# Six feature blocks ahead of the first projection, and one first phase of two passes

## The chip, the cores and the metric

The kernel runs on one core of a Trainium2 chip. The metric is the device time of one execution in microseconds (us), the median of three runs. The engines are TensorE (PE: matmuls and transposes, PEld: weight loads beside them), VectorE (DVE), ScalarE (ACT), GpSimd (POOL) and SyncE (SP), which issues nearly all transfers from the chip's memory (HBM) to the on-chip memory (SBUF). Matmuls write into eight banks of PSUM.

## The reference

Two transformer blocks on 256 tokens of width 2048, in float32. The first mixes with two kinds of attention (stick-breaking, and sparse with an indexer that keeps the 64 best keys per query), the second with gated linear attention (GLA); each has a gated feed-forward part. What matters here is the beginning of the first block:

```python
c_act = jax.nn.silu(c)
mod = c_act @ w_ada[l] + b_ada[l]                 # 2048 x 12288
sh1, sc1, gt1, sh2, sc2, gt2 = jnp.split(mod, 6, axis=-1)
h = modulate(rms_norm(x, g_mix[l]), sh1, sc1)     # h * (1 + sc1) + sh1
z = h @ w_in[l]                                   # 2048 x 11344
(q_sb, k_sb, v_sb, q_ds, k_ds, v_ds, q_ix, k_ix, w_ix,
 gate_sb, gate_ds) = split_columns(z)             # 1024 wide each, k_ix 64, w_ix 16, gates 2048
o_sb = stick_breaking_attention(q_sb, k_sb, v_sb) # 8 heads
o_ds = indexer_sparse_attention(q_ds, k_ds, v_ds, q_ix, k_ix, w_ix * (N_IDX_HEADS ** -0.5), rel_bias)
merged = (jax.nn.sigmoid(gate_sb) * (o_sb @ w_o_sb[l])
          + jax.nn.sigmoid(gate_ds) * (o_ds @ w_o_dsa[l]))
x = x + gt1[:, None, :] * (merged @ w_out[l])
...                                               # feed-forward with sh2, sc2, gt2, then the second block
```

So no projection can start before the columns of w_ada for sh1 and sc1 have been read and summed, at least those of the features that the projection multiplies first.

## The kernel before

**Halves.** All large weights come through one path. A half is 512 KB of weights: two blocks of 128 features by 512 columns. SP reads it into one of eight places of `raw` (L294 or, in the first phase, L335), ScalarE rounds it to a high part `whi` (L1014), VectorE subtracts to get the low part `wlo` (L1586), and TensorE multiplies the 256 tokens with 12 matmuls of 512 columns: high by high, high by low, low by high (`half`, L472, its matmuls L482 to L484). There are 896 halves. `whi` and `wlo` have four places, so the two splitting engines can be four halves ahead of TensorE; SP issues a half's transfer once the low part of the half eight before is made (`lo_made`). Two halves are a slab.

**The modulation.** c @ w_ada is done on VectorE: one row block of w_ada at a time is multiplied by its entry of c_act and added to a sum (L1681 and L1691 for the first columns, L1702 for later ones, L1606 for the rest). The sums over 128 partitions are then turned into columns by small matmuls with ones (`first_columns`, L567). For sh1 and sc1 the 16 feature blocks stand in two parts: the first EARLY = 10 blocks come in 16 pieces of 1280 KB (`early_piece`, L321) ahead of any projection, the other six in 16 pieces of 768 KB (`late_piece`, L327) beside the first halves. The pieces go through SLOTS = 4 places.

**The phases.** A (48 halves) computes q, k, v of the stick-breaking part in six groups of 512 columns: a first pass over the ten early blocks of all six groups (30 halves), then a second over the other six blocks (18 halves). Partial sums that don't fit into PSUM are drained after the first pass and added after the second. B (4 x 16 halves) computes q, k, v of the sparse part and the queries of the indexer; beside its halves the eight stick-breaking heads run, one per eight halves. C1 (32 halves, from half 112 on, slabs 56 to 71) computes the first gate, and beside it the indexer's scores are added up; in its last slabs eight rounds of top-k (L1866, L1867) run on VectorE, one per half split. C2 (32 halves from half 144 on, slabs 72 to 87) computes the second gate beside the sparse heads: scores, softmax on VectorE (`soft`, which ends at L1903), turned probabilities (L709), values. O, U and the feed-forward parts follow.

**The other w_ada columns.** The columns for sh2, sc2, gt1 and gt2 come in chunks of 512 KB (`ada_chunk`, L306, two places), added by L1606. A table, CHUNKS_AT, says after which slab SP issues which chunk; the add stands in VectorE's program behind the split of that slab's second half. SP waits, before it issues chunk n, for the add of chunk n - 2, and all that SP issues is one line of instructions.

**The distance loads.** `hankels` (L374) is 16 loads of bias tables per head from a small DRAM scratch (L380, L382), in SP's line after a slab of C1; the sparse heads' softmax uses them.

**Warming up.** Ahead of the first projection TensorE runs matmuls whose result is not used (`keep_running`, L573), between the transposes of X (L516) and the column sums.

Of the kernel before, what the change touches and what calls it, by code (L numbers as in the profile page):

```python
# [37 lines left out]
for _h in range(GH):  # L38
# [43 lines left out]
def build_program(nc, A, out):  # L82
# [205 lines left out]
    def _(sp):  # L288
# [57 lines left out]
        for i in range(48):  # L346
            first_half(i)
            if i == 2 * RING - 1:
                for kt in range(SLOTS):
# [4 lines left out]
            if i == 28:
                sp.dma_start(ixw_raw[:].rearrange("p (k n) -> p k n", k=KT), w_in[:, :, C_IX:C_IX + NIXW]).then_inc(sem("ixw_in"), 16)
            if i % 2:
                for n in CHUNKS_AT.get(i // 2, ()):
# [107 lines left out]
    def _(pe):  # L465
# [2138 lines left out]
```

## Time and profile before

| | us |
|---|---|
| runs | 2686.44, 2686.55, 2687.0; median 2686.55 |
| profiled execution, span | 2684.8 |
| TensorE busy | 2629.5 (98%) |
| VectorE busy | 1794.2 (67%) |
| ScalarE busy | 1290.9 (48%) |
| first projection matmul | starts at 70.06 |

The profile is of one execution. Its times count from the start of the span, which is the time from the first to the last instruction that it shows; a run's time is a little longer. The granted clock is the share of full speed at which TensorE was allowed to run. An idle time in brackets stands behind the engine that had it, with what ended it; a wait of TensorE is one that its matmuls had, and SPq is SP's issuing of a transfer, not the transfer.

### The profile page before, as it was taken

Reading aid. Unit: us, or ns where it says so; the run is one execution under the profiler, and the core shown is the slowest. Engines: PE = TensorE matmul, PEld = TensorE weight load, DVE = VectorE, ACT = ScalarE, POOL = GpSimd, SP = SyncE. Lnnn points to the kernel's source line nnn. Section 1 sums busy time; section 2 is a strip of 40 time slices with the busy share of each in tenths; the row PEclk is TensorE's granted clock in tenths of the full one; section 3 lists DMA queues with packets and bytes.
Section 4 is the critical chain, followed back from the end, with each engine's and each line's share of the span. In section 5 each row is a group of like instructions: output and inputs, shape, how many; then the busy total and the mean of one; then the engine's idle time right before and its main releaser. Section 6 shows DMA issues by size and latency. Waiting matters only on the chain.

```text
span 2684.8 us, 34364 instructions
## 1 busy us (share of the span) xinstructions
PE 2629.5 (98%) x12051; PEld 2166.7 (81%) x12051; DVE 1794.2 (67%) x2061; ACT 1290.9 (48%) x1558; POOL 228.6 (9%) x164
## 2 busy tenths in 40 slices
PE   2999999999999999999999999999999999999999
PEld 1887887888888888888888887887888888888887
DVE  7977776878777666666666865677555555555554
ACT  2545554445455444444444564556554444444443
POOL 0000000100000000000000310130001111111110
PEclk9999999999999999999999999999999999999999
DMA  9978777677786666666666556643666666666663
GB/s 391 389 269 301 270 259 256 209 251 264 291 286 230 205 202 205 202 204 203 203 203 189 188 172 184 190 145 126 203 186 191 188 192 190 188 192 190 189 194 134
DMA packets 280529, 585.56 MB, mean 218 GB/s; under 512 B 21776, under 2 KB 24236, under 8 KB 279540
## 3 DMA queue, kind: packets, MB, share of 16 engines
q1 hardware_dynamic: 280084, 583.61, 67.0%
q8 instruction: 58, 0.95, 0.1%
q10 hardware_dynamic: 352, 0.71, 0.1%
q14 instruction: 35, 0.29, 0.0%
HBM read 582.07 MB, written 2.11 MB: 218 GB/s over the span
## 4 chain that ended last, share of the span: by engine, by line
PE 94%; DVE 3%; DMA 1%; issue 1%; ACT 0%; SPq 0%; DVEq 0%; ACTq 0%
PE lin L482 29%; PE lin L484 29%; PE lin L483 29%; DVE sb_acc L1681 1%; DMA sb_raw<-in_w_in_dram 1%; PE aux L785 1%; DMA sb_ada<-in_w_ada_dram 1%; PE aux L516 1%; PE aux L959 0%; PE aux L573 0%; PE aux L796 0%; DVE sb_wlo L1586 0%; PE aux L482 0%; PE aux L484 0%; PE aux L483 0%
## 5 line engine op out<-in xcount | busy, mean ns | idle before, releaser
L1586 DVE TENSOR_TENSOR sb_wlo<-sb_raw,sb_whi 128x1024 fp32r<-128x1024 f32 x896 | 1103.6, 1236 | 781.0 <-ACT sb_whi L1014 777.6
L1014 ACT ACTIVATE sb_whi<-sb_raw 128x1024 fp32r<-128x1024 f32 x896 | 948.0, 1060 | 1219.6 <-PE lin L484 1134.9
L482 PE MATMUL lin<-sb_whi,sb_act_hi 128*128 128x512 f32 x2636 | 1045.1, 396 | 1.8 <-DVE sb_wlo L1586 1.0
L484 PE MATMUL lin<-sb_whi,sb_act_lo 128*128 128x512 f32 x2636 | 1027.4, 390 | 0.0
L483 PE MATMUL lin<-sb_wlo,sb_act_hi 128*128 128x512 f32 x2636 | 1026.3, 389 | 0.0
L482 PEld LDWEIGHTS lin<-sb_whi,sb_act_hi 128*128 128x128 f32 x2636 | 495.2, 188 | 107.0 <-issue 8.7
L484 PEld LDWEIGHTS lin<-sb_whi,sb_act_lo 128*128 128x128 f32 x2636 | 494.7, 188 | 104.6
L483 PEld LDWEIGHTS lin<-sb_wlo,sb_act_hi 128*128 128x128 f32 x2636 | 495.5, 188 | 100.2 <-issue 2.2
L482 PE MATMUL lin<-sb_whi,sb_hid_hi 128*128 128x512 f32 x704 | 275.4, 391 | 0.0
L484 PE MATMUL lin<-sb_whi,sb_hid_lo 128*128 128x512 f32 x704 | 274.2, 389 | 0.0
L483 PE MATMUL lin<-sb_wlo,sb_hid_hi 128*128 128x512 f32 x704 | 273.9, 389 | 0.0
L484 PEld LDWEIGHTS lin<-sb_whi,sb_hid_lo 128*128 128x128 f32 x704 | 132.1, 188 | 27.7
L483 PEld LDWEIGHTS lin<-sb_wlo,sb_hid_hi 128*128 128x128 f32 x704 | 132.2, 188 | 27.0
L482 PEld LDWEIGHTS lin<-sb_whi,sb_hid_hi 128*128 128x128 f32 x704 | 132.2, 188 | 27.0
L1606 DVE SCALAR_TENSOR_TENSOR sb_ada_acc<-sb_ada_in,sb_small,sb_ada_acc 128x1024 f32<-128x1024 f32 x90 | 115.1, 1279 | 0.7 <-DVE sb_u_lo L1659 0.7
L2489 POOL TENSOR_TENSOR sb_yacc<-sb_yacc,sb_dstage 128x512 f32<-128x512 f32 x36 | 55.6, 1545 | 556.8 <-ACT sb_dstage L1028 556.8
L2489 POOL TENSOR_TENSOR sb_x<-sb_x,sb_dstage 128x512 f32<-128x512 f32 x36 | 63.6, 1766 | 336.3 <-ACT sb_dstage L1028 336.3
L2468 POOL TENSOR_TENSOR sb_hank<-sb_hank,sb_selneg 128x384 f32<-128x384 f32 x8 | 11.7, 1492 | 516.4 <-DVE sb_selneg L1880 516.4
L2495 POOL TENSOR_TENSOR sb_ubuf<-sb_ubuf,sb_cacc 128x512 f32<-128x512 f32 x11 | 18.1, 1647 | 397.7 <-ACT sb_ubuf L1028 397.7
L2097 DVE SCALAR_TENSOR_TENSOR sb_cacc<-sb_gpad,sb_par,sb_cacc 128x256 f32<-128x256 f32 x88 | 48.1, 588 | 5.7 <-DVE sb_cacc L2097 1.4
L482 PE MATMUL lin<-sb_whi,sb_u_hi 128*128 128x512 f32 x128 | 51.0, 398 | 0.0
L484 PE MATMUL lin<-sb_whi,sb_u_lo 128*128 128x512 f32 x128 | 49.9, 390 | 0.0
(360 smaller groups left out, 1804.8 us busy)
## 6 DMA issues: line engine op xcount, KB each, us to landing
sb_raw<-in_w_in_dram SPq DMA_DIRECT2D x176, 512.0 KB, 5.9
sb_raw<-in_ffn_w_gu_dram SPq DMA_DIRECT2D x176, 512.0 KB, 3.7
sb_ada_in<-in_w_ada_dram SPq DMA_DIRECT2D x128, 512.0 KB, 4.1
sb_raw<-in_gla_w_in_dram SPq DMA_DIRECT2D x96, 512.0 KB, 3.8
sb_raw<-in_w_gate_dram SPq DMA_DIRECT2D x88, 512.0 KB, 3.8
sb_raw<-in_w_up_dram SPq DMA_DIRECT2D x88, 512.0 KB, 4.4
sb_raw<-in_w_down_dram SPq DMA_DIRECT2D x88, 512.0 KB, 5.6
sb_raw<-in_ffn_w_down_dram SPq DMA_DIRECT2D x88, 512.0 KB, 3.6
```

The lines of the kernel that those rows point to most:

```text
L482: pe.matmul(o, h, whi[:, w], start=first and q == 0, stop=False)
L483: pe.matmul(o, h, wlo[:, w], start=False, stop=False)
L484: m = pe.matmul(o, l, whi[:, w], start=False, stop=last and q == 1)
L516: m = pe.transpose(aux[n % 4][:, q * S + tb * P:q * S + (tb + 1) * P], src[:, tb, (2 * g + q) * P:(2 * g + q + 1) * P], ident)
L785: m = pe.transpose(aux[f // 2][:, f % 2 * S + tb * P:f % 2 * S + (tb + 1) * P], src[:, tb, f * P:(f + 1) * P], ident)
L1014: act.activation(whi[:, idx % RING * HALF:(idx % RING + 1) * HALF], raw[:, idx // 2 % RING, idx % 2 * HALF:(idx % 2 + 1) * HALF], ACT.Copy ...
L1586: dve.tensor_tensor(wlo[:, c], raw[:, idx // 2 % RING, idx % 2 * HALF:(idx % 2 + 1) * HALF], whi[:, c].bitcast(fp32), ALU.subtract).then_i ...
L1606: dve.scalar_tensor_tensor(acc[:, c], ada_in[:, half, :], cact[:, ds(kt, 1)], acc[:, c], ALU.mult, ALU.add).then_inc(sem("ada_sum"), 1)
L1681: m = dve.scalar_tensor_tensor(acc, new, cact[:, kt:kt + 1], acc, ALU.mult, ALU.add)
L2097: m = dve.scalar_tensor_tensor(cacc[:, f, :], gpad[:, f, 2 - k:2 - k + S], col(w, f), cacc[:, f, :], ALU.mult, ALU.add)
L2489: pool.tensor_tensor(y[:, 0, s], y[:, 0, s], dstage[:, c % 2, :], ALU.add).then_inc(sem("dstage_free"), 1)
L2495: pool.tensor_tensor(ubuf[:, 0, :], ubuf[:, 0, :], cacc[:].rearrange("p a t -> p (a t)")[:, 0:NB], ALU.mult).then_inc(sem("up_mul"), 1)
```

## The change

EARLY goes from 10 to 6 and SLOTS from 4 to 6. The early pieces have 768 KB; the ten late blocks come in 32 half rows of 640 KB (sh1 and sc1 apart) beside halves 4 to 35, in six places. Phases A and B become one phase A of 112 halves in 14 groups: a first pass over three pairs of blocks for all groups (42 halves), a second over the other five pairs (70 halves). The heads stand in the second pass, one per seven halves from half 55 on. The third column sum has 40 small matmuls with 16 columns, before 24 with 32, and comes after half 38, before after half 25. Partial sums of the first pass are both drained on ScalarE and both added on VectorE. The `ada_columns` sums move from the end of B into C1, after its halves 13 and 15. `hankels` comes after slab 68, before after slab 64. The table of chunks is another one. The scaling of X comes after the add of block 6, before of block 7.

```diff
-EARLY = 10
+EARLY = 6
-SLOTS = 4
+SLOTS = 6
+LATE_SLOTS = 6
...
-    ("A", 1, 48, 9), ("B", 4, 16, 2), ("C1", 1, 32, 4), ...
+    ("A", 1, 112, 25), ("C1", 1, 32, 4), ...
...
-LATE_AT = {}
-for _k in range(KT):
-    LATE_AT.setdefault(A_PAIRS + 4 * _k // 3, []).append(_k)
+LATE_SUMMED = 38
+LATE_PAIRS = 41
+HEADS_AT = [55 + 7 * _h for _h in range(NH)]
...
 for _n in range(110):
-    _at = 14 + _n * 10 // 16 if _n < 16 else 24 + (_n - 16) * 6 // 7 if _n < 44 else 4 + _n if _n < 64 else 11 + _n if _n < 96 else 13 + _n if _n < 107 else 17 + _n
+    _at = 23 + _n * 33 // 20 if _n < 20 else 56 + (_n - 20) // 2 if _n < 32 else 62 + (_n - 32) * 44 // 64 if _n < 96 else 13 + _n if _n < 107 else 17 + _n
...
-        def late_piece(kt):
-
-            sp.wait_ge(sem("ada0_sum"), EARLY_ROWS if kt < SLOTS else EARLY_ROWS + kt - SLOTS + 1)
-            sp.dma_start(ada1[:, kt % SLOTS, :].rearrange("p (b n) -> p b n", b=2), w_first[kt * P:(kt + 1) * P, :, EARLY * P:D]
-                         ).then_inc(sem(f"ada0_in{kt % SLOTS}"), 16)
+        def late_piece(n):
+
+            kt, b = n // 2, n % 2
+            if n >= LATE_SLOTS:
+                sp.wait_ge(sem("ada0_sum"), EARLY_ROWS + n - LATE_SLOTS + 1)
+            else:
+                if n == 0:
+                    sp.wait_ge(sem("tt_T"), KT // 2)
+                sp.wait_ge(sem("ada0_sum"), KT - SLOTS + n + 1)
+            sp.dma_start(ada1[n % LATE_SLOTS][:], w_ada[kt * P:(kt + 1) * P, b * D + EARLY * P:(b + 1) * D]).then_inc(...)
...
-                if after and s == 0:
+                if after and s == 4:
                     after()
...
-            acc, c0, w = (acc1, 0, KT - EARLY) if n == 2 else (acc0, k0 * P, k1 - k0)
+            acc, c0, w, wide = (acc1, 0, KT - EARLY, WIDE // 4) if n == 2 else (acc0, k0 * P, k1 - k0, WIDE // 2)
...
+        for i, (g, p) in enumerate(A_HALVES):
+            again = i >= A_FIRST
...
+            if i == LATE_SUMMED:
+                pe.wait_ge(sem("ada0_sum"), EARLY_ROWS + 2 * KT)
+                first_columns(2)
+            if i == A_ENDS[0] - 1:
+                project_ix()
+            if i == A_ENDS[1]:
+                wix_turn()
+            for h, at in enumerate(HEADS_AT):
+                if i == at:
+                    sb_turn(h)
+                if i == at + 2:
+                    sb_scores(h)
+                if i == at + 5:
+                    sb_suffix(h)
+                if i == at + 7:
+                    sb_values(h)
...
+            if idx in (13, 15):
+                pe.wait_ge(sem("sb_out"), NH)
+                ada_columns(idx // 15)
...
-            if kt == 7:
+            if kt == 6:
                 norm_stats(0)
                 norm_rows(X)
...
         def a_sum(n):
 
             drained(0, "A", A_ENDS[n])
             for tb, free in ((0, free0), (1, free1)):
-                dve.wait_ge(free, 2 + 3 + n)
-                z = sbz[:, tb, g * NB:(g + 1) * NB]
-                dve.tensor_tensor(z, banks[tb][:], z, ALU.add).then_inc(free, 1)
+                dve.wait_ge(free, 2 + GROUPS - A_HELD + n)
+                z = projected(A_AGAIN[n], tb)
+                dve.tensor_tensor(z, lin[n % 2][tb][:], z, ALU.add).then_inc(free, 1)
...
+        for n in range(2 * KT):
+            hk.setdefault(RING + n, []).append(lambda n=n: late_add(n))
```

On SP, at the start: w_ada pieces (`sb_ada`), the first halves (`sb_raw`) and X (`sb_x`) before,

```order
L321 DMA sb_ada_56<-in_w_ada_dram 128x2x1280 x4
L341 DMA sb_x<-in_x_dram 128x2x2048
...
L321 DMA sb_ada_56<-in_w_ada_dram 128x2x1280 x12
L335 DMA sb_raw<-in_w_in_dram 128x2x512 x8
L327 DMA sb_ada_57<-in_w_ada_dram 128x2x768 x4
L335 DMA sb_raw<-in_w_in_dram 128x2x512 x6
L327 DMA sb_ada_57<-in_w_ada_dram 128x2x768
```

and now:

```order
L328 DMA sb_ada_56<-in_w_ada_dram 128x2x768 x4
L353 DMA sb_x<-in_x_dram 128x2x2048
...
L328 DMA sb_ada_56<-in_w_ada_dram 128x2x768 x12
L347 DMA sb_raw<-in_w_in_dram 128x2x512 x5
L340 DMA sb_ada_0_57<-in_w_ada_dram 128x1280
L347 DMA sb_raw<-in_w_in_dram 128x2x512
L340 DMA sb_ada_1_58<-in_w_ada_dram 128x1280
```

The early pieces are shorter, and from the fifth half on a half row of the late columns stands between every two halves.

On SP, in C1 around the distance loads (`sb_hank`; a row of `sb_raw` x2 is a slab, a row of `sb_ada_in` its chunk): before, the slab ahead of the loads is halves 128 and 129, the one behind them 130 and 131,

```order
L294 DMA sb_raw<-in_w_in_dram 128x2x512 x2
L306 DMA sb_ada_in<-in_w_ada_dram 128x1024
L294 DMA sb_raw<-in_w_in_dram 128x2x512 x2
L306 DMA sb_ada_in<-in_w_ada_dram 128x1024
L380 DMA sb_hank<-bias_by_distance 128x256
...
L294 DMA sb_raw<-in_w_in_dram 128x2x512 x2
```

and now halves 136 and 137, and 138 and 139:

```order
L299 DMA sb_raw<-in_w_in_dram 128x2x512 x2
L313 DMA sb_ada_in<-in_w_ada_dram 128x1024
L299 DMA sb_raw<-in_w_in_dram 128x2x512 x2
L313 DMA sb_ada_in<-in_w_ada_dram 128x1024 x2
L386 DMA sb_hank<-bias_by_distance 128x256
...
L299 DMA sb_raw<-in_w_in_dram 128x2x512 x2
```

The slab ahead of the loads has two chunks (41 and 42) where it had one (60), and the slab before it one (40).

On VectorE, the beginning of top-k: splits (`sb_wlo`), and rounds on `sb_selneg`. Before, from the split of half 140 on,

```order
L1586 TENSOR_TENSOR sb_wlo<-sb_raw,sb_whi 128x1024
L1866 MAX sb_top_77<-sb_selneg 128x8
L1867 MATCH_REPLACE sb_selneg<-sb_top_77,sb_selneg 128x128
L1866 MAX sb_top_77<-sb_selneg 128x8
L1867 MATCH_REPLACE sb_selneg<-sb_top_77,sb_selneg 128x256
L1586 TENSOR_TENSOR sb_wlo<-sb_raw,sb_whi 128x1024
```

and now, with adds of chunks to `sb_ada_acc` between:

```order
L1616 SCALAR_TENSOR_TENSOR sb_ada_acc<-sb_ada_in,sb_small,sb_ada_acc 128x1024
L1596 TENSOR_TENSOR sb_wlo<-sb_raw,sb_whi 128x1024
L1861 MAX sb_top_82<-sb_selneg 128x8
L1862 MATCH_REPLACE sb_selneg<-sb_top_82,sb_selneg 128x128
L1861 MAX sb_top_82<-sb_selneg 128x8
L1862 MATCH_REPLACE sb_selneg<-sb_top_82,sb_selneg 128x256
L1596 TENSOR_TENSOR sb_wlo<-sb_raw,sb_whi 128x1024
L1861 MAX sb_top_82<-sb_selneg 128x8
L1862 MATCH_REPLACE sb_selneg<-sb_top_82,sb_selneg 128x128
L1861 MAX sb_top_82<-sb_selneg 128x8
L1862 MATCH_REPLACE sb_selneg<-sb_top_82,sb_selneg 128x256
L1616 SCALAR_TENSOR_TENSOR sb_ada_acc<-sb_ada_in,sb_small,sb_ada_acc 128x1024 x2
```

Between half 138 and the first softmax eight such adds stand now, and none before.

## Rows read from the trace of the kernel before

**Rows 1.** Waits of TensorE, 66 to 2690 us: total, times, longest

```profile
PE aux L628 <- ACT sb_qk_sb L1151: 1.2, 1, 1.2
```

**Rows 2.** The page's head

```profile
span 2684.8 us, 34364 instructions
```

**Rows 3.** Stretches: busy PE, PEld, DVE, ACT, POOL (count), PEclk, DMA share, GB/s

```profile
40.00:60.00 20.00, 9.52 (x36) 7.50 (x37) 19.07 (x10) 6.77 (x10) 0.00 (x0) 0.78 1.02 414
...
80.00:100.00 20.00, 20.00 (x90) 16.57 (x89) 20.00 (x16) 8.86 (x10) 0.00 (x0) 1.00 1.05 392
...
120.00:140.00 20.00, 20.00 (x90) 16.58 (x89) 16.18 (x13) 8.20 (x8) 0.00 (x0) 1.00 1.03 363
```

**Rows 4.** Order in time, the start: start, length, what, [idle before <- releaser]

```profile
42.64 6.20 PE L516 MATMUL aux<-sb_con,sb_x 128*128 128x128 f32 x32 [15.39 <-ACT sb_x L1046]
...
56.68 7.76 PE L573 MATMUL aux<-sb_con 128*128 128x512 f32 x12 [7.84 <-DVE sb_acc L1681]
...
62.62 3.02 DVE L1691 SCALAR_TENSOR_TENSOR sb_acc<-sb_ada,sb_small,sb_acc 128x1024 f32<-128x1024 f32 x2
...
66.92 2.76 PE L567 MATMUL aux<-sb_con,sb_acc 128*128 128x32 f32 x24
...
70.06 0.80 PE L482 MATMUL lin<-sb_whi,sb_act_hi 128*128 128x512 f32 x1
```

**Rows 5.** Order in time, VectorE around the loads and top-k

```profile
444.75 1.22 DVE L1586 TENSOR_TENSOR sb_wlo<-sb_raw,sb_whi 128x1024 fp32r<-128x1024 f32 x1 [0.87 <-ACT sb_whi L1014]
...
464.24 1.23 DVE L1586 TENSOR_TENSOR sb_wlo<-sb_raw,sb_whi 128x1024 fp32r<-128x1024 f32 x1 [4.59 <-ACT sb_whi L1014]
...
476.24 1.23 DVE L1586 TENSOR_TENSOR sb_wlo<-sb_raw,sb_whi 128x1024 fp32r<-128x1024 f32 x1 [0.22 <-ACT sb_whi L1014]
...
488.46 1.23 DVE L1586 TENSOR_TENSOR sb_wlo<-sb_raw,sb_whi 128x1024 fp32r<-128x1024 f32 x1 [1.49 <-ACT sb_whi L1014]
...
524.10 1.56 DVE L1903 TENSOR_SCALAR sb_lg<-sb_lg,sb_small 128x128 f32<-128x128 f32 x2
```

**Rows 6.** Order in time, TensorE: first matmuls of halves 135, 138, 139; probabilities

```profile
484.39 0.39 PE L482 MATMUL lin<-sb_whi,sb_act_hi 128*128 128x512 f32 x1
...
493.65 0.39 PE L482 MATMUL lin<-sb_whi,sb_act_hi 128*128 128x512 f32 x1
...
496.37 0.39 PE L482 MATMUL lin<-sb_whi,sb_act_hi 128*128 128x512 f32 x1
...
527.94 0.49 PE L709 MATMUL aux<-sb_con,sb_lg 128*128 128x128 f32 x3
```

**Rows 7.** Groups of VectorE, 60 to 240 us: busy, mean ns, idle before

```profile
L1586 DVE TENSOR_TENSOR sb_wlo<-sb_raw,sb_whi 128x1024 fp32r<-128x1024 f32 x60 | 72.7, 1221 | 16.1 <-ACT sb_whi L1014 15.6
L1702 DVE SCALAR_TENSOR_TENSOR sb_acc<-sb_ada,sb_small,sb_acc 128x1536 f32<-128x1536 f32 x15 | 27.2, 1815 | 2.1 <-DMA sb_ada<-in_w_ada_dram 2.1
L1606 DVE SCALAR_TENSOR_TENSOR sb_ada_first<-sb_ada_in,sb_small,sb_ada_first 128x1024 f32<-128x1024 f32 x21 | 26.5, 1279 | 1.2 <-DMA sb_ada_in<-in_w_ada_dram 1.2
```

**Rows 8.** Transfers issued, 0 to 160 us: KB each, median us to landing

```profile
sb_ada<-in_w_ada_dram SPq DMA_DIRECT2D x16, 1280.0 KB, 9.7
sb_raw<-in_w_in_dram SPq DMA_DIRECT2D x36, 512.0 KB, 11.4
sb_ada<-in_w_ada_dram SPq DMA_DIRECT2D x16, 768.0 KB, 11.9
```

**Rows 9.** A stretch of phase B, columns as in rows 3

```profile
230.00:390.00 160.00, 160.00 (x747) 133.37 (x747) 125.11 (x135) 90.82 (x107) 0.00 (x0) 1.00 0.77 267
```

**Rows 10.** Order in time, SP around the distance loads

```profile
447.19 0.34 SPq L306 DMA_DIRECT2D sb_ada_in<-in_w_ada_dram  x1
...
454.98 0.43 SPq L382 DMA_DIRECT2D sb_hank<-bias_by_distance  x1
455.45 0.94 SPq L294 DMA_DIRECT2D sb_raw<-in_w_in_dram  x2
```

**Rows 11.** Order in time, ScalarE: the high part of half 130

```profile
463.14 1.06 ACT L1014 ACTIVATE sb_whi<-sb_raw 128x1024 fp32r<-128x1024 f32 x1 [5.95 <-DMA sb_raw<-in_w_in_dram]
```

**Rows 12.** Waits of VectorE, 530 to 700 us: total, times, longest

```profile
DVE sb_wlo L1586 <- ACT sb_whi L1014: 25.2, 26, 2.3
```

More of the change, by code:

```diff
@@ L643, in sb_values @@
             pe.matmul(aux[3][:, 0:S], head_of(sbz, 2, 0, h), lb[:, 0:S], start=True, stop=False)
-            pe.matmul(aux[3][:, P:S], head_of(sbz, 2, 1, h), lb[:, S:S + P], start=False, stop=True).then_inc(sem("sb_o"), 1)
-        def sb_hooks(it):
-            def run(idx):
-                for off, step in ((0, sb_turn), (2, sb_scores), (5, sb_suffix), (7, sb_values)):
-                    if idx % 8 == off:
-                        step(2 * it + idx // 8, idx // 8)
-                if isinstance(it, int) and it == 3 and idx in (11, 13):
-                    pe.wait_ge(sem("sb_out"), NH - 1)
-                    ada_columns(idx // 13)
-            return run
@@ L656, in _ @@
-        pe.wait_ge(sem("wix_made"), 1)
-        def b_body(it):
-            for k in range(2):
-                group(it, "B", 16, 2, 8 * k, k, 8, sb_hooks(it))
-        for it in range(4):
-            b_body(it)
+            pe.matmul(aux[3][:, P:S], head_of(sbz, 2, 1, h), lb[:, S:S + P], start=False, stop=True).then_inc(sem("head_o"), 1)
+        first_banks = (lin[1], lin[0], aux[2:4])
+        for i, (g, p) in enumerate(A_HALVES):
+            again = i >= A_FIRST
+            n = (i - A_FIRST) // (KT // 2 - A_PAIRS) if again else i // A_PAIRS
+            held = n < A_HELD if again else n >= GROUPS - A_HELD
+            banks = first_banks[(GROUPS - A_HELD + n) % 3] if again and held else lin[n % 2] if again else first_banks[n % 3]
+            if p == (A_PAIRS if again else 0) and not (again and held):
+                pe.wait_ge(free0, 12 + n if again else n)
+                pe.wait_ge(free1, 12 + n if again else n)
+            if n == 0:
+                pe.wait_ge(sem("tt_lo"), p + 1)
+            half(0, "A", A_ENDS[-1], i, 0, 2 * p, p == (0 if held or not again else A_PAIRS), p == (KT // 2 - 1 if held or again else A_PAIRS - 1),
+                 banks=banks)
+            if i == LATE_SUMMED:
[14 more added lines that the diff above has]
+                    sb_values(h)
@@ new lines, in weights, with hold_out @@
+        def weights(h):
+            act.wait_ge(sem("sb_sm"), h + 1)
+            act.activation(lb[:], lb[:], ACT.Exp).then_inc(sem("sb_ex"), 1)
+        def hold_out(h):
+            act.wait_ge(sem("head_o"), h + 1)
+            act.activation(oT_sb[:, h, :], aux[3][:, 0:S], ACT.Copy).then_inc(sem("sb_out"), 1)
+        for h, at in enumerate(HEADS_AT):
+            for off, step in ((4, hold_qk), (6, softplus), (9, weights), (11, hold_out)):
+                hk.setdefault(at + off, []).append(lambda h=h, step=step: step(h))
@@ L1180, in hold_q @@
+        body(0, "A", A_ENDS[-1], hk, start=RING)
         def hold_q(p):
@@ L1751, in _ @@
             if g < RING:
-                split(0, "A", 48, g)
+                split(0, "A", A_ENDS[-1], g)
             first_low(g, xT[:, 2 * g:2 * g + 2, :])
+        for idx in range(A_PAIRS, RING):
+            split(0, "A", A_ENDS[-1], idx)
         pairs[0] = KT // 2
@@ new lines, in _ @@
+        hk = {A_ENDS[n] + 3: [lambda n=n: held_drain(n) if n < A_HELD else a_sum(n)] for n in range(GROUPS)}
+        for n in range(2 * KT):
+            hk.setdefault(RING + n, []).append(lambda n=n: late_add(n))
+        for g in range(A_PAIRS, KT // 2):
+            hk.setdefault(LATE_PAIRS + g - A_PAIRS, []).append(lambda g=g: late_low(g))
+        hk.setdefault(LATE_PAIRS + KT // 2 - A_PAIRS, []).append(split_ix)
+        hk.setdefault(A_ENDS[1] + 3, []).append(hold_wix)
+        SC = HD ** -0.5
@@ new lines, in weights @@
+        def weights(h):
+            dve.wait_ge(sem("sb_suf"), h + 1)
+            dve.tensor_tensor(lb[:], lb[:], aux[2][:, 0:3 * P], ALU.add).then_inc(sem("sb_sm"), 1)
+            dve.wait_ge(sem("sb_ex"), h + 1)
+            dve.tensor_tensor(lb[:], lb[:], sbmask, ALU.mult).then_inc(sem("sb_a"), 1)
+        for h, at in enumerate(HEADS_AT):
+            hk.setdefault(at + 6, []).append(lambda h=h: log_keep(h))
+            hk.setdefault(at + 9, []).append(lambda h=h: weights(h))
+        body(0, "A", A_ENDS[-1], hk, start=RING)
```

282 lines of the change are left out of this document (114 added, 168 removed).

## The prediction, on record before the changed kernel ran

> **What bounds the kernel now.** I read the waits of TensorE first, then stretches of 20 us at the start, then the order in time around the two places that move. From 66 us on TensorE waits for almost nothing: the largest entry in its list is 1.2 us [rows 1], in a span of 2684.8 us [rows 2]. So after the start an instruction taken from another engine is worth nothing, and one added there is free until the lead of VectorE over TensorE is used up. Before 66 us the transfers are the bound: from 40 to 60 us TensorE is busy 9.52 of 20 us while the queue moves 414 GB/s [rows 3], and the first projection matmul starts at 70.06 [rows 4]. The reader is to see two prices in this: bytes that must land before 70.06 cost their full time, and what comes later costs only what exceeds a lead.
>
> **The lead.** ScalarE and VectorE split each half of weights up to four halves ahead of the matmuls. Half 135 is split from 476.24 on and multiplied from 484.39 [rows 5, 6]; with 1.22 us for a split [rows 7] the lead is 484.39 - 477.46 = 6.9 us. The split of half 139 starts at 488.46, after VectorE had stood idle for 1.49 us waiting for ScalarE [rows 5], so here the ring caps the lead; half 139 begins at 496.37 [rows 6], and has 6.7 us of it.
>
> **1. The start.** Sixteen pieces of 1280 KB [rows 8] become 768 KB, which takes 16 x 512 KB = 8.39 MB out of the queue ahead of the first projection. At 414 GB/s [rows 3] that is 20.3 us. Against it, smaller transfers may run slower: with 512 and 768 KB mixed [rows 8], 80 to 100 us shows 392 GB/s [rows 3]. What is left to move (16 x 768 KB, X and the constants, 15.3 MB) would then take 39.0 instead of 37.0 us, and the gain is 18.2. No row is nearer to one end than to the other, so I take the middle, **-19.3**, and the first projection at about 50.8. Is something else late there? The transposes of X start at 42.64 and take 6.2 us [rows 4]. X is scaled behind the add of block 6 now, not 7: eight pieces of 1280 KB ahead of that become seven of 768, 5.0 MB or 12 us less, so the transposes end near 36.8, and the warm-up matmuls, at 56.68 before [rows 4], come at 37.4. They are just in time. TensorE stood for 7.84 us ahead of them [rows 4], and the mean granted clock of that stretch is 0.78 [rows 3]; now the pause is about gone, so the clock costs nothing, and what it gives back lies under the transfers.
>
> **2. The third column sum.** It had 24 small matmuls with 32 columns out, now 40 with 16. The 24 took 2.76 us [rows 4], 0.115 each, with nothing beside them, so 16 more are **+1.8** on TensorE; if the narrower output is cheaper in proportion it is 0 (40 x 0.058 against 2.76).
>
> **3. Pass one.** Beside each of halves 4 to 35 stands a half row of 640 KB. The 1.18 MB per half take 3.00 us at 392 GB/s [rows 3], the matmuls 496.37 - 493.65 = 2.72 us [rows 6]. Over 32 halves the queue falls back by 9.0 us. What covers it is its start: VectorE's last early adds begin at 62.62, their data landed, and the projections at 70.06 [rows 4], so 7.4 us of later transfers are in by then. 1.6 is left, and the split lead takes part of it: **+0.8**, bounds 0 and 1.6. VectorE isn't the bound: adds of 1024 and 1536 columns take 1.279 and 1.815 us [rows 7], so one of 1280 about 1.55, and 2.77 with the split where nothing overlaps, as much as TensorE needs.
>
> **4. Pass two with heads.** A head comes each seven halves rather than eight. VectorE was busy 125.11 of 160 us in the old phase B [rows 9], 78%: with h for what a head adds on TensorE, 0.78 x (21.8 + h) us of work in eight halves. Seven halves have one split less (1.2) and sums of two blocks where there was a copy of one (about as much more), so as much work stands against 19.0 + h: less for any h. Cost **0**; the cover is 2 us and more per head, and without it what is over would show at every head. The two ada columns move from B into C1, their matmuls unchanged: 0.
>
> **5. The 16 distance loads.** SP issues them in line, and no weights before they are out. They stand behind a chunk of w_ada that waits for the add two chunks earlier. Before: the chunk at 447.19, after split and add of half 125, the last load at 454.98, the next weights (half 130) at 455.45 [rows 10]; ScalarE gets them at 463.14, after 5.95 us of idling [rows 11], and split 130, begun at 464.24, ends at 465.46. Split 125 began at 444.75 and ended at 445.97 [rows 5]: 19.5 us from end to end. Five halves lay between, and the lead shrank but held. Now two chunks stand in the slab ahead of the loads; the second waits for the add beside half 135, in the slab just before, and the next weights are half 138: three halves on. From half 135 to 138 TensorE needs 493.65 - 484.39 = 9.3 us [rows 6], with the lead 16.2. So split 138 comes 19.5 - 16.2 = **+3.3** late, and the lead is zero from there. Bounds: 0, if the add is earlier than I read, and +4.6 with one more chunk of 0.52 MB at 392 GB/s in the queue.
>
> **6. Top-k without the gap.** Before, slabs 68 to 74 carry no chunk: the eight rounds of top-k stand there. Now there are 1.45 per slab throughout. Between half 138 and the first softmax VectorE gets eight chunk adds more (seven by half 147, one beside 149) of 1.28 us [rows 7]: 10.2. What covers them: the softmax ended at 525.66 (524.10 and 1.56) and TensorE takes it at 527.94 [rows 5, 6], 2.3 spare; and VectorE's idle time in the stretch, the 1.49 at half 139 and some 0.3 in smaller pieces. With the lead in hand 10.2 - 4.1 = 6.1 us of stall; with the 6.7 us gone at half 138, 12.8. With step 5 I take **+12.8**, bounds 6.1 and 12.8.
>
> **7. C2 and O.** VectorE waited 25.2 us for ScalarE's halves from 530 to 700 [rows 12], and gets some 12 adds more there, 15.4 us. The total fits, single places may not: **+1.0**, bounds 0 and 10 (the second rival).
>
> **The sum.** -19.3 + 1.8 + 0.8 + 0 + 3.3 + 12.8 + 1.0 = +0.4. The span of 2684.8 becomes 2685.2; the median of the runs before, 2686.55, lies 1.75 above that span, so 2687 us.
>
> **A rule against step 1.** From 80 to 100 us transfers of 512 and 768 KB ran at 392 GB/s, little under the 414 with 1280 KB [rows 3]. The Trainium skill ("DMA: Bandwidth & Descriptors", section Bandwidth) says to batch transfers to 1 MiB or more for 75% of the peak, and its table has 341 GB/s at 1 MB; cutting 1280 KB to 768 is the wrong way by it. By its 341, an estimate, the 15.3 MB take 44.9 us (7.9 more than at 414) and a half of pass one 3.46 us. This trace stands above that table at either size. The mechanism, priced from rows, is the third rival.
>
> **Rivals.**
> - *The loads' gate doesn't bite* (faster): the add of half 135 falls early enough and the lead stays at 6.7. Step 5 is 0, step 6 is 6.1, step 7 about 0.5: -19.3 + 1.8 + 0.8 + 6.1 + 0.5 = -10.1, 2676 us. For it: before, the same loads cost TensorE no wait [rows 1]. Against it: three halves between, not five. Chance 0.27.
> - *The lead is never regained in C2 and O* (slower): where a slab carries two chunks, SP issues the next weights only after an add three halves earlier. The loop over four halves is then up to 7.7 us from issue to ScalarE (455.45 to 463.14 [rows 10, 11]), 1.06 to split there, 2.4 on VectorE and 1.28 for the add, 12.4 against 10.9 of matmuls: 1.5 us a loop. With the lead at zero it decides wherever two such slabs follow; 14 of 32 slabs have two chunks, and I count six or so loops: 9 instead of 1.0, +8.4 in all, 2695 us. For it: step 5 takes the lead. Against it: the 25.2 us, and without the loads in the queue a landing is shorter than 7.7. Chance 0.20.
> - *The smaller transfers are slow*: at 363 GB/s, as from 120 to 140 us [rows 3], the 15.3 MB take 42.1 us and step 1 is -20.3 + 5.1 = -15.2; a half of pass one takes 3.25, so step 3 is 0.53 x 32 - 7.4 = 9.6. That is 12.9 more than the sum, 2700 us. For it: the change makes every piece smaller. Against it: 392 in the fuller stretch. Chance 0.06.
>
> **Chances.** My forecast 0.45, the rivals 0.27, 0.20, 0.06, and 0.02 for none of these. About 0.2%, 5.4 us, is what a measurement of this kernel can tell from no change. The forecast's own range, 2681 to 2692, lets a tenth out on either side. Faster: 0.25 of the first rival and 0.05. Slower: 0.18 of the second, 0.06 and 0.03. Same: the rest, 0.43. The range for 8 in 10 goes from 4 us under the first rival, 2672, to 2699, short of the third.
>
> **What would show it.** The first projection matmul at 50.8 (step 1 is wrong after 53). No wait of TensorE in pass one. About 3 us of idling before half 138, behind a ScalarE that waits for a transfer; then waits for the low half of the weights and for the softmax, 12 us together, by the first heads of C2; no waits in O. If half 138 has a lead of 5 us or more, step 5 is wrong and the first rival holds; if TensorE waits again and again in C2 and O, the second; if half 35 starts late behind transfers, the third.

## The result and the profile after

The changed kernel takes 2710.74 us (median of four runs, 2707.86 to 2713.67), the kernel before 2686.76 in the same comparison: a ratio of 1.0087, 95% interval 1.0073 to 1.0101. It is 24 us slower; 2687 was forecast and 2699 was the end of the range. The profiled execution has a span of 2706.0 us, 21.2 more than [rows 2]; it was the fastest of the four, so the account below is one of 21.2 us, not of 24.

The way to read it is to lay the start of every half's first matmul beside that of before. From the two traces (this and later tables are worked out from the start of each twelfth projection matmul on TensorE; minus is earlier than before):

| half | where | before | after | difference |
|---|---|---|---|---|
| 0 | first projection | 70.06 | 53.35 | -16.7 |
| 130 | C1, all moved sums done | 469.05 | 455.41 | -13.6 |
| 138 | behind the distance loads | 493.65 | 483.18 | -10.5 |
| 152 | first sparse heads | 535.47 | 540.46 | +5.0 |
| 176 | O begins | 613.79 | 620.62 | +6.8 |
| 216 | in U | 730.18 | 751.20 | +21.0 |
| 860 | near the end | 2581.53 | 2602.73 | +21.2 |

So 34.6 us are lost between halves 130 and 216, against 3.1 between 0 and 130 and 0.2 behind 216. The waits of TensorE, which answer to [rows 1], from 45 us on (total, times, longest):

```profile
PE lin L488 <- DVE sb_wlo L1596: 10.1, 10, 3.0
PE aux L713 <- issue: 8.5, 2, 6.8
PE lin L488 <- DVE sb_u_lo L1669: 6.3, 1, 6.3
PE lin L488 <- DVE sb_act_lo L1909: 1.6, 1, 1.6
```

**The start**, in order of time, against [rows 4]:

```profile
30.35 5.46 PE L522 MATMUL aux<-sb_con,sb_x 128*128 128x128 f32 x32 [7.86 <-ACT sb_x L1058]
...
40.98 7.01 PE L579 MATMUL aux<-sb_con 128*128 128x512 f32 x12 [5.17 <-DVE sb_acc L1691]
...
44.78 1.95 DVE L1701 SCALAR_TENSOR_TENSOR sb_acc<-sb_ada,sb_small,sb_acc 128x1024 f32<-128x1024 f32 x2
...
47.82 1.87 PE L573 MATMUL aux<-sb_con,sb_acc 128*128 128x32 f32 x16
...
53.35 0.47 PE L488 MATMUL lin<-sb_whi,sb_act_hi 128*128 128x512 f32 x1 [0.97 <-DVE sb_wlo L1596]
```

The last early piece lands 19.2 us earlier (62.30 to 43.05 us in the two traces), its adds come only 17.8 us earlier (62.62 to 44.78), and the projections 16.7. Two things lie between. VectorE, which scales X in the middle of the early adds, falls behind the pieces by it. Before, a piece landed every 3.16 us and took 2.98 on VectorE, so VectorE caught up; now one lands every 1.95 us and takes 1.92, and the last add begins 1.7 us after its piece has landed, before 0.3. The adds behind the scaling, before and now, have no idle time of note:

```profile
41.70 20.82 DVE L1681 SCALAR_TENSOR_TENSOR sb_acc<-sb_ada,sb_small,sb_acc 128x2560 f32<-128x2560 f32 x7
```

```profile
29.41 15.27 DVE L1691 SCALAR_TENSOR_TENSOR sb_acc<-sb_ada,sb_small,sb_acc 128x1536 f32<-128x1536 f32 x8
```

And the warm-up (L579) ran until 48 and stood in front of the first column sums, whose data were there at 46.1. It began after a pause of 5.17 us, and stretches of 2 us show what followed the pause (columns as in [rows 3]):

```profile
40.00:42.00 2.00, 1.02 (x2) 0.54 (x3) 1.90 (x2) 0.00 (x0) 0.00 (x0) 0.71 1.03 401
42.00:44.00 2.00, 2.00 (x4) 0.97 (x3) 1.90 (x2) 0.00 (x0) 0.00 (x0) 0.50 1.04 386
44.00:46.00 2.00, 2.00 (x5) 0.77 (x5) 1.90 (x3) 1.06 (x1) 0.00 (x0) 0.94 1.06 388
...
164.00:166.00 2.00, 2.00 (x6) 1.62 (x6) 0.41 (x3) 1.14 (x3) 0.00 (x0) 0.50 0.17 18
```

The granted clock is 0.50 (1.2 GHz) in the first 3 us of the warm-up; and again at 164 us, at the end of the third column sum:

```profile
159.56 4.76 PE L573 MATMUL aux<-sb_con,sb_acc 128*128 128x16 f32 x40
164.15 0.77 PE L488 MATMUL lin<-sb_whi,sb_act_hi 128*128 128x512 f32 x1
```

Half 39, which follows it, takes 4.22 us instead of 2.72.

**Around the distance loads**, SP, then ScalarE, VectorE and TensorE, against [rows 5, 6, 10, 11]:

```profile
460.14 0.95 SPq L299 DMA_DIRECT2D sb_raw<-in_w_in_dram  x2
461.13 4.79 SPq L313 DMA_DIRECT2D sb_ada_in<-in_w_ada_dram  x2
466.03 0.37 SPq L386 DMA_DIRECT2D sb_hank<-bias_by_distance  x1
...
473.09 0.43 SPq L388 DMA_DIRECT2D sb_hank<-bias_by_distance  x1
473.56 0.94 SPq L299 DMA_DIRECT2D sb_raw<-in_w_in_dram  x2
```

```profile
480.81 1.06 ACT L1026 ACTIVATE sb_whi<-sb_raw 128x1024 fp32r<-128x1024 f32 x1 [11.44 <-DMA sb_raw<-in_w_in_dram]
```

```profile
481.90 2.58 DVE L1596 TENSOR_TENSOR sb_wlo<-sb_raw,sb_whi 128x1024 fp32r<-128x1024 f32 x2 [9.15 <-ACT sb_whi L1026]
```

```profile
483.18 0.50 PE L488 MATMUL lin<-sb_whi,sb_act_hi 128*128 128x512 f32 x1 [3.02 <-DVE sb_wlo L1596]
```

The second chunk of the slab is issued after the add beside half 135, the loads after it, and the weights of half 138 reach ScalarE 11.4 us after it ran dry: TensorE waits 3.0 us, and its lead is gone.

**At the first sparse head**, TensorE and VectorE:

```profile
521.46 0.76 PE L713 MATMUL aux<-sb_qk_ds 128*128 128x128 f32 x2 [6.85 <-issue]
...
522.52 0.99 PE L488 MATMUL lin<-sb_whi,sb_act_hi 128*128 128x512 f32 x1
```

```profile
519.81 1.22 DVE L1596 TENSOR_TENSOR sb_wlo<-sb_raw,sb_whi 128x1024 fp32r<-128x1024 f32 x1
...
520.94 0.42 DVE L1882 COPY sb_qk_ds<-aux 128x256 f32<-128x256 f32 x1
```

"issue" hides a semaphore: L713 takes the copy L1882, which stands behind the split of half 148 on VectorE, while L713 stands after half 146 on TensorE. With a lead of two halves that is free. Without it the 6.85 us hold what VectorE has in front of the copy: a round of top-k, two adds of chunks (2.5 us) and the split of half 148.

**In O** SP is the one to look at, then ScalarE:

```profile
655.61 3.81 SPq L313 DMA_DIRECT2D sb_ada_in<-in_w_ada_dram  x2
659.46 0.95 SPq L299 DMA_DIRECT2D sb_raw<-in_w_o_sb_dram  x2
664.65 0.34 SPq L313 DMA_DIRECT2D sb_ada_in<-in_w_ada_dram  x1
665.03 0.95 SPq L299 DMA_DIRECT2D sb_raw<-in_w_o_sb_dram  x2
```

```profile
664.83 1.06 ACT L1026 ACTIVATE sb_whi<-sb_raw 128x1024 fp32r<-128x1024 f32 x1 [5.71 <-DMA sb_raw<-in_w_o_sb_dram]
```

ScalarE's waits from 620 to 740 us, after:

```profile
ACT sb_whi L1026 <- DMA sb_raw<-in_w_o_sb_dram: 27.2, 10, 5.7
ACT sb_whi L1026 <- DMA sb_raw<-in_w_o_dsa_dram: 22.7, 15, 4.4
ACT sb_whi L1026 <- DMA sb_raw<-in_w_out_dram: 11.5, 4, 9.1
ACT sb_whi L1026 <- PE lin L490: 5.1, 4, 2.1
```

and before, in the same halves (613 to 730 us):

```profile
ACT sb_whi L1014 <- PE lin L484: 49.7, 36, 2.1
ACT sb_whi L1014 <- DMA sb_raw<-in_w_out_dram: 4.7, 2, 4.2
```

Before, ScalarE stood at the ring's end and waited for TensorE; now it waits for weights, since SP holds them back behind an add. The longest of these waits comes at U's first half, half 208. On TensorE it shows as a wait for L1669:

```profile
723.94 0.79 PE L488 MATMUL lin<-sb_whi,sb_u_hi 128*128 128x512 f32 x1 [6.34 <-DVE sb_u_lo L1669]
```

But L1669 stands behind the split of half 208 on VectorE, that split waits for ScalarE, ScalarE for the weights, and SP issued these behind a chunk that waited 4.5 us, and behind the read of X (L400):

```profile
704.89 4.46 SPq L313 DMA_DIRECT2D sb_ada_in<-in_w_ada_dram  x2
709.40 0.44 SPq L400 DMA_DIRECT2D sb_x<-in_x_dram  x1
709.88 0.98 SPq L299 DMA_DIRECT2D sb_raw<-in_w_out_dram  x2
```

```profile
720.97 1.06 ACT L1026 ACTIVATE sb_whi<-sb_raw 128x1024 fp32r<-128x1024 f32 x1 [9.07 <-DMA sb_raw<-in_w_out_dram]
```

```profile
722.06 1.23 DVE L1596 TENSOR_TENSOR sb_wlo<-sb_raw,sb_whi 128x1024 fp32r<-128x1024 f32 x1 [4.89 <-ACT sb_whi L1026]
723.20 0.68 DVE L1669 TENSOR_TENSOR sb_u_lo<-aux,sb_u_hi 128x512 fp32r<-128x512 f32 x1
```

So this is the same late line of weights. From the start of half 207 to that of half 208 the kernel loses 6.5 us by it, and in half 208, which runs in part at a granted clock of 0.50, another 1.5.

### The profile page after: what moved, and what is told of

It is laid out like the page before. It is cut to its first block, busy times and chain, and to the rows that moved or that the text cites. A ratio compares the mean times of both kernels' runs of the same rounds, so it can differ in the third digit from the quotient of the medians.

```text
span 2706.0 us, 34402 instructions
## 1 busy us (share of the span) xinstructions
PE 2640.3 (98%) x12051; PEld 2172.0 (80%) x12051; DVE 1799.9 (67%) x2076; ACT 1293.3 (48%) x1570; POOL 228.7 (8%) x164
## 4 chain that ended last, share of the span: by engine, by line
PE 86%; DVE 6%; DMA 4%; issue 2%; ACT 1%; SPq 1%; DVEq 0%; ACTq 0%
PE lin L488 27%; PE lin L490 26%; PE lin L489 26%; DMA sb_raw<-in_w_in_dram 1%; DVE sb_wlo L1596 1%; DMA sb_raw<-in_w_o_sb_dram 1%; DVE sb_ada_acc L1616 1%; ACT sb_whi L1026 1%; PE aux L797 1%; DMA sb_ada_in<-in_w_ada_dram 1%; PE aux L488 1%; PE aux L489 1%; PE aux L490 1%; DMA sb_ada<-in_w_ada_dram 1%; DVE sb_acc L1691 1%
## 5 line engine op out<-in xcount | busy, mean ns | idle before, releaser
L488 PE MATMUL lin<-sb_whi,sb_u_hi 128*128 128x512 f32 x128 | 51.8, 405 | 6.3 <-DVE sb_u_lo L1669 6.3
```

The costliest lines, as they stand in the source:

```text
L488: pe.matmul(o, h, whi[:, w], start=first and q == 0, stop=False)
```

## The experiments

All but one start from the changed kernel. The table gives, for each, the time and the ratio to the kernel before, and TensorE's difference to before at five halves of its profiled execution.

| kernel | us | ratio, 95% | 0 | 130 | 152 | 176 | 216 |
|---|---|---|---|---|---|---|---|
| changed | 2710.74 | 1.0087 (1.0073 to 1.0101) | -16.7 | -13.6 | +5.0 | +6.8 | +21.0 |
| x1_gap | 2698.41 | 1.0040 (1.0026 to 1.0054) | -16.0 | -11.0 | -5.0 | -5.0 | +10.6 |
| x2_thin | 2700.0 | 1.0049 (1.0033 to 1.0066) | -16.3 | -5.3 | +12.1 | +12.1 | +12.1 |
| x3_pool | 2703.12 | 1.0056 (1.0040 to 1.0073) | -16.2 | -11.8 | +8.8 | +10.6 | +16.5 |
| x4_front | 2695.9 | 1.0030 (1.0019 to 1.0042) | -16.8 | +2.2 | +8.5 | +8.5 | +8.5 |
| x5_spread | 2709.7 | 1.0081 (1.0065 to 1.0096) | -15.5 | -11.5 | +6.5 | +8.2 | +22.2 |
| x6_start | 2709.04 | 1.0075 (1.0061 to 1.0088) | -16.9 | -10.0 | +8.2 | +9.9 | +24.0 |
| x8_hankpool | 2708.01 | 1.0076 (1.0060 to 1.0091) | -16.2 | -11.4 | +3.3 | +5.2 | +20.7 |
| x11_two | 2707.98 | 1.0076 (1.0060 to 1.0091) | -16.3 | -12.3 | +2.7 | +4.4 | +21.4 |
| x12_before_dense | 2705.12 | 1.0062 (1.0046 to 1.0077) | -0.4 | +0.8 | +0.8 | +5.3 | +21.5 |
| x9_best | 2683.36 | 0.9985 (0.9976 to 0.9994) | -18.3 | -14.9 | -12.8 | -10.7 | -4.6 |
| x10_best2 | 2680.43 | 0.9972 (0.9962 to 0.9983) | -17.7 | -6.5 | -4.9 | -4.9 | -4.9 |

**x1_gap** takes the chunks out of the top-k stretch:

```diff
-    _at = 23 + _n * 33 // 20 if _n < 20 else 56 + (_n - 20) // 2 if _n < 32 else 62 + (_n - 32) * 44 // 64 if _n < 96 else ...
+    _at = 23 + _n * 33 // 30 if _n < 30 else 56 + (_n - 30) // 2 if _n < 42 else 62 + (_n - 42) * 44 // 64 if _n < 51 else 62 + (_n - 32) * 44 // 64 if _n < 96 else ...
```

> The changed kernel with the 10 chunks of slabs 68 to 74 issued in pass two instead (30 chunks there, not 20); from slab 75 on the table is unchanged, 45 chunks in slabs 75 to 105. Theory: the 18.6 us that the changed kernel loses from half 137 to half 152 come from those adds in the top-k stretch and from the add that holds up the distance loads; they go, and the 14 us lost in O (halves 176 to 208) stay, being made there: about 2692 us. Rival A: O's loss is the lead that was lost at half 138 and never came back; then it goes too, and the time is about 2678 us. Rival B: the distance loads alone did it, adds or not: 2705 us or more.

From half 137 to 152 it loses 6.0 us, not 18.6: no wait at half 138 or in top-k, but a lead of only 1.5 to 3 us, so L713 still waits 2.9. From 176 to 216 it loses 15.6. Rival A (O pays for the lead lost at top-k) falls, rival B too. The total is 6.4 us above the forecast of 2692, which had the loss around top-k go altogether.

**x2_thin** makes C2 and O thin instead:

```diff
...
+    _at = 23 + _n * 33 // 36 if _n < 36 else 56 + (_n - 36) // 2 if _n < 48 else 62 + (_n - 48) * 44 // 64 if _n < 67 else 75 + (_n - 67) * 32 // 29 if _n < 96 else ...
```

> The changed kernel with 16 more chunks in pass two, so that slabs 75 to 105 (C2 and O) carry 29 chunks and not 45, at most one per slab; the chunks of slabs 56 to 74, top-k's among them, are as many per slab as in the changed kernel. Theory: O's 14 us go, because no slab there has two chunks, and the 18.6 us of halves 137 to 152 stay: about 2696 us. Rival A (O's loss follows from the lead lost at half 138): 2709 us or more.

From half 152 to 216 its distance to before stays the same to a few hundredths: C2 and O cost nothing with at most one chunk per slab. The top-k loss stays (17.5 from 130 to 152). The 16 chunks more in pass two cost 8.3 us at half 130, hence 2700 and not 2696.

**x3_pool** leaves every add where it is and takes the wait out of SP's line:

```diff
+POOL_CHUNKS = range(60, 96)
...
             for n in chunks_after(phase, it, per, s):
-                ada_chunk(n)
+                if n not in POOL_CHUNKS:
+                    ada_chunk(n)
...
+        for n in POOL_CHUNKS:
+            pool.wait_ge(sem("ada_sum"), n - 1)
+            kt, half, piece = n % 32 // 2, n % 2, ADA_PIECES[n // 32]
+            pool.dma_start(ada_in[:, half, :], ...).then_inc(sem(f"pool_come{half}"), 16)
```

> The changed kernel with chunks 60 to 95 (slabs 81 to 105) issued by GpSimd rather than SP: the same adds on VectorE at the same places, but SP's line of weights no longer stands behind a wait for an add. Theory: what O loses is late weights, since SP waits in line; its 14 us shrink to under 4, total about 2700 us. Rival C: VectorE has too many adds in O; nothing changes, 2711 us.

The loss from half 176 to 216 goes from 14.2 to 5.9, with the same adds; the forecast was under 4. Of the 8.3 us saved 6.8 are at U's first half, whose wait on TensorE goes from 6.34 to 0.88 us. ScalarE's waits from 620 to 740 us:

```profile
ACT sb_whi L1030 <- PE lin L494: 57.9, 36, 5.0
ACT sb_whi L1030 <- issue: 3.6, 1, 3.6
```

No wait for weights is left: the line on SP made them late. Of the 5.9 the larger part is one wait of VectorE for a chunk, 4.5 us: the chunk was issued at 688.88, while the read of X was under way, and took 8.9 us to land. Rival C (too many adds) falls for 8.3 us of the 14.2.

**x12_before_dense** puts the suspected cause alone into the kernel before:

```diff
-... else 4 + _n if _n < 64 else 11 + _n if _n < 96 else ...
+... else 4 + _n if _n < 51 else 62 + (_n - 32) * 44 // 64 if _n < 96 else ...
```

> The kernel before with one edit: chunks 51 to 95 take the changed kernel's places in slabs 75 to 105 (1.45 per slab, so that every other slab or so has two); chunks up to 50 and the gap of slabs 68 to 74 as before. Theory: two chunks in a slab put SP's line of weights behind an add only three halves ahead, whatever came before, and that alone costs 10 to 15 us in O: about 2699 us. Rival: O's loss needs something else of the changed kernel (its phase A, or the lead lost at top-k): within 4 us of before.

It loses 20.8 us between halves 152 and 216, of them 16.2 in O and at U's first half, from a full lead at top-k (6.7 us at half 138). That is more than the 10 to 15 us of the theory; 4.6 us are already lost in C2. ScalarE, 620 to 740 us:

```profile
ACT sb_whi L1014 <- DMA sb_raw<-in_w_o_sb_dram: 28.7, 11, 5.9
ACT sb_whi L1014 <- DMA sb_raw<-in_w_o_dsa_dram: 23.4, 15, 4.4
ACT sb_whi L1014 <- DMA sb_raw<-in_w_out_dram: 9.4, 3, 8.5
ACT sb_whi L1014 <- PE lin L484: 7.3, 4, 2.1
```

The same rows as in the changed kernel. The density of chunks from slab 75 on is enough by itself; the rest of the change isn't needed for it.

**x4_front** has all 64 chunks before top-k and the old table after it (`23 + _n * 33 // 43`, `56 + (_n - 43) * 12 // 21`, then `11 + _n`).

> The changed kernel with chunks 0 to 63 in slabs 23 to 67 (43 in pass two, 21 in the first 12 slabs of C1), none in slabs 68 to 74, and one per slab from 75 on as in the kernel before. Theory: both losses go and only the 13.6 us of gain up to half 130 is left: about 2674 us, faster than the kernel before. Rival D: pass two with heads has no room for 23 more adds (29 us of VectorE) and pays 10 us or more there: 2684 us or more.

O is free, but pass two pays: +2.2 at half 130 instead of -13.6, rival D. The cover of a head, which the forecast put at 2 us, isn't enough for 43 chunks in 33 slabs. Around top-k it still loses 6.2 us without a chunk there, as x1 loses 6.0.

**x5_spread, x8_hankpool, x11_two** deal with the distance loads: two heads after each of four slabs; all 16 from GpSimd; two transfers in place of 16.

```diff
-                if after and s == 4:
-                    after()
+                if after and s >= 4:
+                    after(s - 4)
...
-            for h in range(NH):
+            for h in (2 * part, 2 * part + 1):
```

> The changed kernel with the 16 distance loads spread over four slabs, two heads after each of slabs 68 to 71, on SP as before; all else as changed. Theory: the 3.2 us of idling before half 138 come from the 7.8 us that the 16 issues take in one place; they go, and some of the lead (2 to 4 us) lives on into top-k: about 2704 us. Rival: the adds of top-k eat whatever lead there is, and PE just waits later, by the same sum: 2710 us.

```diff
-        def hankels():
...
-            cols_body(it, "C1", C_GATE, hankels if it else None)
+            cols_body(it, "C1", C_GATE, None)
...
+        pool.wait_ge(sem("ada_T"), 1)
+        for h in range(NH):
...
+            pool.dma_start(hank[:, h, P:3 * P], ...).then_inc(sem("hank_in"), 16)
...
+            pool.dma_start(hank[:, h, 0:P], ...).then_inc(sem("hank_in"), 16)
```

> The changed kernel with the 16 distance loads issued by GpSimd, so that SP's line of weights never stands behind them; table of chunks unchanged. Theory: no wait before half 138, a lead of 6 us there, of which the chunk adds in top-k take all: the loss from half 137 to 152 falls from 18.6 to some 6 to 8 us, O's loss of 14 stays, about 2700 us. Rival: it only moves, 2707 us or more.

```diff
-            for h in range(NH):
...
+            for c0, w, to in ((0, S, slice(P, 3 * P)), (P, P, slice(0, P))):
...
+                sp.dma_start(hank[:, :, to], bass.AP(..., ap=[[1, P], [2 * S, NH], [1, w]])).then_inc(sem("hank_in"), 16)
```

> The changed kernel with the distance loads as two transfers for all eight heads rather than 16, same place in SP's line, same bytes. If the 7.8 us of issuing on SP made the wait before half 138, it goes (lead there 3 us or more). If the transfers themselves did (4096 short rows in the queue, as the two kernels with the loads spread or issued by GpSimd suggest, whose lead at half 138 was 0.8), the lead at half 138 is under 1.5 us all the same. Total 2705 to 2711 us either way, since the adds of top-k eat what lead there is.

In all three the wait before half 138 is gone (the difference to before stays level from 137 to 139), as the theory had it. But the lead there is 0.5 to 0.8 us in each, so it isn't the 16 issues on SP in one place that take it. The transfers of the loads are left (2048 rows of 512 and 1024 bytes in the trace, not the 4096 put on record) and the wait for an add in slab 68, which all three keep; these runs don't part the two. The adds of top-k take the rest: L713 waits 6.9 us in all three, and the times can't be told from the changed kernel's. My theory for x5 and x8, that a lead would live on, fell; the rival of each was right. What the loads take, issues and transfers together, without a chunk beside them can be read from x1 and x4, which have none in slabs 68 to 74: the lead falls from 6.9 us at half 137 to 1.9 at half 138 in x1, and from 5.7 to 0.4 in x4.

**x6_start** moves the warm-up forward and cuts the third column sum in two:

```diff
...
-        pe.wait_ge(sem("ada0_sum"), KT - 3)
-        keep_running(5)
+        pe.wait_ge(sem("ada0_sum"), KT - 5)
+        keep_running(7)
...
-                first_columns(2)
+                first_columns(2, 0)
+            if i == LATE_SUMMED + 1:
+                first_columns(2, 1)
```

> The changed kernel with two edits at TensorE's clock: the warm-up begins two adds earlier and with 7 matmuls, not 5, and the 20 small matmuls of the third column sum stand in two lots of 10, after halves 38 and 39. Theory: the first projection starts at 51.4 rather than 53.4, since the warm-up was itself late (TensorE had stood for 5.2 us and ran it at 1.2 GHz), and half 39 takes 2.8 us plus its lot, not 4.2: 1.4 us less. In all 3 us less, up to O; then about 2707 us. Rival: the start is bound by the transfers and the clock falls all the same: 2710 us, first projection at 53.

The second edit works: from half 38 to 40 it loses 4.4 us to before, not 6.1. The first one didn't here, as the rival had it: the first projection came at 53.2. The clock held from 38 us on and fell later, at the sums, so the first projections themselves ran at 1.2 GHz:

```profile
48.00:50.00 2.00, 2.00 (x7) 1.48 (x7) 0.97 (x5) 0.58 (x2) 0.00 (x0) 0.50 1.05 407
50.00:52.00 2.00, 2.00 (x9) 1.48 (x8) 1.54 (x3) 2.00 (x5) 0.00 (x0) 0.50 1.06 403
```

In x9 and x10, with the same two edits, the first projection came at 51.8 and 52.4 us and ran at full speed. Whether the edit holds the clock is thus open; the total is within the interval of the changed kernel.

**x9_best and x10_best2** put together what the others showed. x9 is x1's table, loads and chunks 60 to 95 from GpSimd, and the edits of x6. x10 is x4's table with chunks 0 to 63 issued by GpSimd, the loads as two transfers after slab 69, and the edits of x6.

> All in one: the table of x1 (no chunk in slabs 68 to 74), the distance loads and chunks 60 to 95 issued by GpSimd, and the two edits at the start. Theory: 11.0 us of gain are left at half 137 in x1, 3 more come from the start, top-k costs nothing with its lead, and O costs 4 to 6: about 2678 us, faster than the kernel before. Rival: the start's gain is lost again in pass two, and O costs 10: 2686 us.

> The table of x4 (43 chunks in pass two, 21 in C1 up to slab 67, none in 68 to 74, one per slab from 75), chunks 0 to 63 issued by GpSimd, the distance loads as two transfers after slab 69, and the two edits at the start. In x4 pass two lost 16 us, with ScalarE waiting 46 us for transfers. Theory: most of that was SP's line behind adds; with GpSimd issuing, pass two and C1 lose 5 us or less against the changed kernel, O loses nothing: about 2677 us. Rival: pass two's VectorE is full with 23 more adds; it loses 12 us or more as in x4: 2686 us.

Both beat both kernels: x9 by 0.15% and x10 by 0.28% against before. With the loads off SP's line or in two transfers and no chunk beside them, the loss from half 137 to 152 is 1.5 and 1.6 us, where x1 and x4 lose 6.0 and 6.2. x9 misses its 2678 by 5 us: from half 137 to 152 it loses that 1.5, in C2 another 2.2, and 6.1 from there to 216. x10 pays nothing in O and 1.6 us around top-k. It still pays in pass two and C1: from half 48 to 130, where all have done the same work as before, it loses 10.2 us against before, x4 16.5 and the changed kernel 0.5. So of the 16.0 us that x4 lost more than the changed kernel, GpSimd's issuing took away 6.3. The other 9.7 show mostly as waits of TensorE for VectorE's part of the heads; whether the adds themselves make them or the chunks, for which VectorE waits 18.0 us in that stretch, isn't shown. Its theory, 5 us or less, was half right, and 2677 was 3 us too low.

## Why the prediction was wrong, step by step

- **Step 7 is the step that failed.** It put +1.0 on C2 and O; they cost 8.0 (from +5.0 at half 152 to +13.0 at half 207), within its bounds of 0 and 10 but far from the term taken, and U's first half, for which no step had a term, 8.0 more. The cover named was VectorE's: 25.2 us of waits [rows 12] for 15.4 us of adds. That much was true, VectorE had the time. But what cost was in the main not the adds; it was SP's wait for them, in front of the weights: 8.3 of the 14.2 us behind half 176 go when GpSimd waits in its place (x3), and the places of the chunks alone bring the loss into the kernel before (x12). A cover on one engine was set against a wait on another. What makes the 1.8 us of C2 stays open. The second rival had this loop, at 0.20. Its 9 us for C2 and O were about right; what it lacked is U's first half, whose weights stand behind such a chunk and the read of X: 6.5 us, and 1.5 of cold clock behind that. And its condition was wrong: the lead need not be at zero beforehand (x12), O brings it there by itself.
- **Step 1** was 2.6 us too good: 16.7, not 19.3, and the first projection at 53.35, beyond the 53 that the prediction named as its sign of being wrong. The transfers gave what was forecast, 19.2. 1.4 was VectorE, still behind the pieces from the scaling of X: the prediction asked what else is late there and looked at the transposes, not at VectorE's adds. 1.1 was the warm-up, which I had at nothing since the pause of TensorE would go. It shrank to 5.17 us instead, and the clock fell to 0.50 behind it.
- **The rule against step 1** did not decide: with 640 KB and 512 KB pieces, pass one moved

```profile
80.00:100.00 20.00, 20.00 (x90) 16.58 (x89) 19.77 (x16) 9.65 (x13) 0.00 (x0) 1.00 1.03 401
...
120.00:140.00 20.00, 20.00 (x90) 16.58 (x89) 18.72 (x15) 10.04 (x14) 0.00 (x0) 1.00 1.03 401
```

  401 GB/s, above the 392 and 363 of [rows 3] with larger pieces. The third rival falls. The Trainium skill ("DMA: Bandwidth & Descriptors", section Bandwidth) has 341 GB/s at 1 MB, for transfers that GpSimd issues. This trace, where SP issues them, is above that with smaller pieces.
- **Step 2**, +1.8: right in its own size (4.76 us for 40, so 0.119 each, as for 32 columns); the cold half behind it, 1.5 us, was missing.
- **Step 3**, +0.8: no wait in pass one, the difference goes from -16.7 to -17.0 by half 24. That is 0.3 beyond the lower of its bounds.
- **Step 4**, 0: about right for this table (0.5 us from half 48 to 130); the cover claimed for it was too large, as x2 and x4 showed.
- **Step 5**, +3.3: 3.2, in the place named. But the 7.8 us on SP are only a part of its cause (x5, x8, x11), and the second chunk isn't all of it either: without it the loads still take 5.1 us of the lead (x1).
- **Step 6**, +12.8: 15.5, from -10.5 to +5.0. Waits make some 11 of it, and the longest shows at the scores (L713) rather than the softmax, 6.85 us. The other 4.5 are halves 138, 142 and 147, each in part at half clock behind a wait (half 147 takes 4.69 us for 3.29); the sum had no term for that.
- **The total**: +0.4 was forecast for the span, +21.2 came. Step 7, with U's first half, is 15.0 of that, step 1 2.6, step 6 2.7, the cold half in step 2 1.5, and -1.0 the others together. The range was too narrow because its end had the loop's price for C2 and O but nothing for what the same late weights cost at U's first half, and because steps 1, 2 and 6 missed to the same side.

## What to carry to other kernels

Where one engine issues all transfers in program order, a wait for a small buffer is a wait for everything behind it; count from the awaited instruction to the next transfer in that line and compare that distance, not the busy time of the engine awaited. Another engine with little to do can take such an issue over, with the work at the same places; here that gave 8.3 us back for the chunks behind half 176 (x3) and nothing for the distance loads by themselves (x8). And a lead that is lost is paid at each place where the program counts on it, as at L713 in x1 and x4, so look for the next such place before giving the sum. A releaser in the profile is the last link only: follow it back, as from L1669 to SP, before naming the cause.

## What the hardware showed beyond expectation

- 40 small matmuls in a row, 4.76 us in which TensorE was busy throughout, were followed by a granted clock of 0.50 at 164 us and six projection matmuls at a pitch of 0.43 us; the 24 of the kernel before were not. Cut into two lots with a half between them (x6), the loss was 1.7 us less. All eight profiled kernels with the 40 in one row show 0.50 there, and none of the three with two lots (x6, x9, x10).
- A small matmul with 16 columns out took as long as one with 32: 0.119 and 0.115 us.
- The runs of the changed kernel spread over 5.8 us, those of before over 0.6 in the same comparison; in later comparisons before ran from 2685.5 to 2691.9.
